# Hybrid decoder layer on one Trainium2 core: a second query block computed in the opening, every third low part made by GpSimd, modulation pieces and column sums placed at other points

## Chip, cores and metric

The kernel runs on 1 core of one Trainium2 chip. The metric is the device time of one execution in microseconds (us), lower is better. The kernel before was timed in three runs; their median is the number to compare with.

## What is computed

One decoder layer for 256 positions (SEQ) of width 2048 (D), all in f32. A conditioning vector `c` gives six vectors of 2048 (shift, scale and gate of the first norm, then of the second) through a matrix `w_ada` of 2048 x 12288, which is 96 MB. This modulation is the part that the change is most about.

```python
mod = (silu(c) @ w_ada + b_ada)
sh1, sc1, g1, sh2, sc2, g2 = split(mod, 6)
h = rmsnorm(x, norm1_g) * (1.0 + sc1) + sh1
sq, sk, sv, cq, ckv, kr = split(h @ w_in, IN_SPLITS)   # 1024, 1024, 1024, 512, 256, 64 columns
sb_out = stick_breaking_attention(sq, sk, sv)          # 8 heads of 128
q = rmsnorm(cq) @ w_uq;  kv = rmsnorm(ckv) @ w_ukv     # latent attention, 8 heads, 64 rotary columns
mla_out = mla_attention(q_nope, rope(q_pe), k_nope, rope(kr), v)
x = x + g1 * (concat(rmsnorm(sb_out), rmsnorm(mla_out)) @ w_o)
h2 = rmsnorm(x, norm2_g) * (1.0 + sc2) + sh2
x = x + g2 * peer_ffn(h2, ...)      # scores against keys, top 16 of 16384 experts for each of 8 heads
return rmsnorm(x, final_norm_g)
```

## The kernel before

Five engines each run a program written out by hand (one block per engine, from L675, L748, L846, L1244 and L1631 on), and wait for each other on semaphores. The order of the work is the order of the Python loops in these blocks: nothing is moved by a scheduler. TensorE (PE) multiplies, VectorE (DVE) and ScalarE (ACT) do elementwise work, SyncE (SP) and GpSimd (POOL) issue DMAs from their own queues. Eight banks of PSUM are handed out round by round with `plan`, `take`, `fill`, `full` and `empty` (L211 to L231). The stages are these.

**Opening (7 to 149 us).** Shift and scale of the first norm are needed ahead of any input product. Their part of `w_ada` comes as 64 pieces of 512 KB (`first_load`, L467, 14 buffers), 16 pieces for each quarter j of the columns. DVE adds them up, weighted by silu(c), in `first_acc` (`first_step`, L474 to L487). PE turns the sum of 128 partitions into columns by products with a vector of ones (`summed_columns`, L492, 8 matmuls for a quarter), and DVE and ACT apply them to the four 128-row chunks of `hT` of this quarter. Then PE multiplies the chunks, in whole f32, with the first input blocks, `OPENING = ("cq", "ckv", "q0")`: cq and ckv in L876, q0 in L882 (a block of 512 columns of `w_in`; each quarter comes in a tile `opened` of up to 1 MB). SP issues all these loads in one row: the opened tiles of a quarter with the 512 KB pieces of the next one between them.

**Input products (149 to 270 us).** The other blocks, q1, k0, k1, v0, v1, each have 8 pairs of chunks; a pair is counted by c (0 to 39). The weights come in halves of 2 MB in two ring slots (`load_half`, L360). f32 is split in two fp32r parts: ACT makes the high part (L448, four buffers `win_high`), DVE the low part, whole minus high (L452, 128x1024 at a time). PE then multiplies high part by high, weight high by `hT_low`, and weight low by `hT_high`: 24 matmuls of 256 columns for a pair of q or k (L912), 12 of 512 for a pair of v (L906). One record of the trace is one such matmul; a matmul in whole f32 has two records.

**The later modulation** (gate 1, shift 2, scale 2, gate 2) is pieces 32 to 95 of 1 MB, part = piece/16, in three buffers `ada_late` (the last three pieces in `ada_last`). The GpSimd queue issues them (`ada_load`, L302, DMA at L308); piece k waits until sum k-3 is done. DVE adds them up (`ada_sum`, L310; L319 for the first of a part, L322 for the others). PE sums the partitions when 16 pieces are done (`ada_cols(part)`, L329, matmuls L333, 16 for a part: 2 is gate 1, 3 is shift 2, 4 is scale 2), and DVE adds the bias (`ada_finish`, L339). At which points of DVE's program the sums stand is a table: `ada_after` (L513) for the input products, up to piece 58; then 59 to 63, and 64 to 70 (`ADA_IN = 71`) ahead of attention; 13 in the output products, at the pairs listed in the DVE block; the rest ahead of retrieval (`ADA_OUT = 86` is where the next list begins). `ada_cols(3)` stands behind the products `qpe` of the latent queries, `ada_cols(4)` in the output products, item 2, pair 2.

**Latent up-projections and attention (270 to 370 us).** `qpe` is rotated by DVE, then come scores, weights and values of 16 jobs on PE, ACT and DVE.

**Output products (370 to 461 us).** `w_o` in four items n of 8 pairs m, with the same split: high by ACT, low by DVE (L452), 12 matmuls of 512 for a pair (L1069), which is 2.72 us. `residual` (L1896, L1902, L1904) adds the result of the item before, twice in each item from 1 on. **Retrieval** is the rest, up to the end at 1749 us; the change does not touch it beyond the sums of modulation ahead of it.

## Time and profile before

| | |
|---|---|
| three runs | 1755.42, 1748.83, 1753.72 us |
| median | 1753.72 us |
| profiled execution, device time | 1751.18 us |
| its span (first to last instruction) | 1749.4 us |
| mean granted clock of TensorE | 0.909 of full speed |
| matmul, PE | 1478.3 us busy, 85% |
| VectorE | 1206.5 us busy, 69% |
| GpSimd | 690.7 us busy, 39% |
| ScalarE | 542.8 us busy, 31% |
| DMA | 624.46 MB in packets of the queues, mean 357 GB/s |

The profile is of one execution. Its times count from the span's start, and busy shares are means over all stages. GpSimd's time is nearly all in the gathers of the retrieval: before 520 us it does little but issue the modulation pieces. The granted clock is 1.00 where TensorE runs at 2.4 GHz. A row of the timeline joins instructions that follow each other; its last number in brackets is the idle time before them and what ended it.

### The profile page before, as it was taken

The numbers are of one execution on the slowest core, as the hardware profiler recorded it, in microseconds if no ns is written. First come the engines' busy times: TensorE is split into PE (matmuls) and PEld (weight loads), VectorE is DVE, ScalarE is ACT, GpSimd is POOL, SyncE is SP. The second block draws the span as 40 slices with busy tenths as digits, with TensorE's granted clock in tenths as the row PEclk, the third lists the DMA queues.
The fourth block names the chain that finished last, engine by engine and source line by source line (L and its number), as shares of the span: only waits on it lengthen the run. The fifth ranks groups of instructions, "written<-read, shape, count | busy, mean of one in ns | idle before, by whom it ended". The sixth has DMA issues, their size and how long they took to land.

```text
span 1749.4 us, 20157 instructions
## 1 busy us (share of the span) xinstructions
PE 1478.3 (85%) x7320; PEld 980.5 (56%) x7320; DVE 1206.5 (69%) x2134; ACT 542.8 (31%) x1589; POOL 690.7 (39%) x626
## 2 busy tenths in 40 slices
PE   2979999989999998898999757656689899988874
PEld 2558987878788875666676434324333343333331
DVE  5877886879889988898454467768654555445463
ACT  3003442764311247343210146537421010101132
POOL 1000011000122354556676466555654454445461
PEclk9889999999999999999999876667789999998987
DMA  9999997849969679999999899998989999999996
GB/s 337 386 385 407 402 354 308 303 167 370 380 233 359 225 293 379 377 368 397 390 402 396 325 388 379 378 350 319 394 338 406 366 402 400 362 417 389 416 381 249
DMA packets 149806, 624.46 MB, mean 357 GB/s; under 512 B 33994, under 2 KB 38272, under 8 KB 86528
## 3 DMA queue, kind: packets, MB, share of 16 engines
q0 software_dynamic: 82976, 427.52, 62.6%
q1 hardware_dynamic: 66732, 195.67, 29.1%
q8 instruction: 58, 0.95, 0.2%
q14 instruction: 40, 0.33, 0.0%
HBM read 797.54 MB, written 2.10 MB: 457 GB/s over the span
## 4 chain that ended last, share of the span: by engine, by line
PE 31%; DMA 30%; DVE 24%; issue 6%; POOL 5%; ACT 3%; DVEq 1%; SPq 1%; POOLq 0%; ACTq 0%
DMA u_rows<-in_peer_u,expert 23%; DVE u_rows L2033 12%; PE ps L1167 6%; PE ps L1069 5%; PE ps L457 4%; PE ps L912 4%; DVE first_acc L486 3%; DMA v_rows<-in_peer_v,expert_rows 3%; POOL v_rows L801 3%; PE ps L906 2%; PE ps L1219 2%; PE ps L1134 2%; DMA ada_first<-in_w_ada 2%; PE ps L1204 2%; DMA u_rows<-in_peer_v,expert_rows 1%
## 5 line engine op out<-in xcount | busy, mean ns | idle before, releaser
L2033 DVE SCALAR_TENSOR_TENSOR u_rows<-u_rows,h 128x1024 f32<-128x1024 f32 (+1 forms) x416 | 595.3, 1469 | 377.9 <-DMA u_rows<-in_peer_u,expert 374.3
L801 POOL DMA_INDIRECT u_rows<-in_peer_u,expert x256 | 320.6, 1253 | 364.5 <-DVE u_rows L2033 289.5
L801 POOL DMA_INDIRECT v_rows<-in_peer_v,expert_rows x199 | 264.1, 1327 | 162.3 <-PE ps L1167 108.5
L1167 PE MATMUL ps<-v_rows,diag 128*32 128x512 f32 x1592 | 259.4, 693 | 65.1 <-DMA v_rows<-in_peer_v,expert_rows 35.6
L1219 PE MATMUL ps<-dense_rows,dense_weight 128*128 128x512 f32 x640 | 290.6, 612 | 14.9 <-DVE dense_sums L2112 8.2
L457 PE MATMUL ps<-h2T,dense_rows 128*128 128x256 f32 x1280 | 284.0, 383 | 4.2 <-ACT dense_weight L1565 4.1
L457 PEld LDWEIGHTS ps<-h2T,dense_rows 128*128 128x128 f32 x1280 | 243.4, 191 | 52.6 <-issue 17.9
L1219 PEld LDWEIGHTS ps<-dense_rows,dense_weight 128*128 128x128 f32 x640 | 123.1, 196 | 181.9 <-issue 174.9
L1167 PEld LDWEIGHTS ps<-v_rows,diag 128*32 128x32 f32 x1592 | 64.9, 125 | 182.5 <-issue 182.0
L308 POOL DMA_DIRECT2D ada_late<-in_w_ada x61 | 32.4, 531 | 303.7 <-DVE ada_acc L322 260.8
L1204 PE MATMUL ps<-high_hot,low_hot 128*128 128x40 f32 x512 | 82.1, 332 | 78.7 <-issue 54.0
L322 DVE SCALAR_TENSOR_TENSOR ada_acc<-ada_late,cact,ada_acc 128x2048 f32<-128x2048 f32 x57 | 133.8, 2348 | 18.8 <-DMA ada_late<-in_w_ada 17.7
L1167 PE MATMUL ps<-spare_rows,diag 128*32 128x512 f32 x296 | 135.7, 673 | 9.7 <-DMA v_rows<-in_peer_v,expert_rows 9.7
L1204 PEld LDWEIGHTS ps<-high_hot,low_hot 128*128 128x128 f32 x512 | 78.9, 244 | 95.0 <-issue 95.0
L1134 PE MATMUL ps<-h2T,ring 128*128 128x256 f32 x512 | 114.2, 383 | 0.0
L1134 PEld LDWEIGHTS ps<-h2T,ring 128*128 128x128 f32 x512 | 97.4, 192 | 13.0
L1487 ACT ACTIVATE hidden<-hidden 128x16 f32<-128x16 f32 x15 | 3.2, 215 | 314.6 <-DVE hidden L2041 311.5
L1576 ACT ACTIVATE low_hot<-iota,slot_rows 128x128 f32<-128x128 f32 x256 | 78.1, 387 | 41.1 <-PE ps L1204 40.9
L486 DVE SCALAR_TENSOR_TENSOR first_acc<-ada_first,cact,first_acc 128x1024 f32<-128x1024 f32 x60 | 77.0, 1284 | 16.1 <-DMA ada_first<-in_w_ada 10.8
L1509 ACT COPY weight_rows<-kept 32x4 f32<-32x4 f32 x240 | 47.1, 196 | 109.4 <-DVE kept L2058 106.7
L1561 ACT ACTIVATE diag<-ident,weight_rows 128x32 f32<-128x32 f32 x256 | 58.6, 308 | 40.0 <-PE ps L1167 39.4
L448 ACT CAST win_high<-ring 128x1024 fp32r<-128x1024 f32 x40 | 41.8, 1052 | 74.4 <-DMA ring<-in_w_in 32.0
(308 smaller groups left out, 1874.1 us busy)
## 6 DMA issues: line engine op xcount, KB each, us to landing
ada_late<-in_w_ada POOLq DMA_DIRECT2D x61, 1024.0 KB, 7.8
dense_rows<-in_dense_u SPq DMA_DIRECT2D x40, 1024.0 KB, 8.9
dense_rows<-in_dense_v SPq DMA_DIRECT2D x40, 1024.0 KB, 9.0
ada_first<-in_w_ada SPq DMA_DIRECT2D x64, 512.0 KB, 11.6
ring<-in_w_in SPq DMA_DIRECT2D x10, 2048.0 KB, 23.8
ring<-in_w_o SPq DMA_DIRECT2D x8, 2048.0 KB, 16.8
ring<-in_w_peer_q SPq DMA_DIRECT2D x8, 2048.0 KB, 13.8
opened<-in_w_in SPq DMA_DIRECT2D x8, 1024.0 KB, 13.0
```

Source lines behind the costliest of these rows:

```text
L322: nc.vector.scalar_tensor_tensor(out=a, in0=piece, scalar=cact[:, kc:kc + 1], in1=a, op0=ALU.mult, op1=ALU.add).then_inc(ada_steps, 1)
L457: ins = nc.tensor.matmul(half, lhs(k), rhs(k), start=(k == 0), stop=(k == kc - 1))
L486: nc.vector.scalar_tensor_tensor(out=a, in0=piece, scalar=cact[:, kc:kc + 1], in1=a, op0=ALU.mult, op1=ALU.add).then_inc(first_steps, 1)
L801: nc.gpsimd.indirect_dma_start(buf[:, :], None, table, bass.IndirectOffsetOnAxis(ap=places, axis=0), bounds_check=last_sparse, oob_is_err= ...
L912: ins = nc.tensor.matmul(banks[b // 2][:, T * (b % 2):T * (b % 2) + T], w.of(part, k, P * b, P), h[:, ch, :], start=first and b % 2 == 0, ...
L1069: ins = nc.tensor.matmul(banks[t], mixed[:, h, P * t:P * t + P], w.of(part, k), start=h % H == 0 and part is w.high and mixed is mix_high_ ...
L1134: ins = nc.tensor.matmul(bank[:, T * s:T * s + T], ring[item[name][0]][:, lo:lo + P], h2T[:, ch, :], start=(ch == 0 and s == 0), stop=(ch ...
L1167: ins = nc.tensor.matmul(ps[rows, k, :], diag[n % len(diag)][:, :], v_slot(n)[0][:, 512 * k:512 * k + 512], start=first, stop=last)
L1204: ins = nc.tensor.matmul(o, low_hot[i % 2][:, k, :], high_hot[i % 2][:, k, :], start=True, stop=True)
L1219: ins = nc.tensor.matmul(ps[:, 4 + t, :], weight_tile(PIECE * m + a)[:, P * t:P * t + P], rows[:, 512 * a:512 * a + 512], start=m == 0 and ...
L1576: ins = nc.scalar.activation(hot[:, k, :], iota128[:, :], ACT.Abs, scale=-1.0, bias=slot_rows[:, 1, BATCH * b + k:BATCH * b + k + 1])
L2033: ins = nc.vector.scalar_tensor_tensor(out=u_rows[b][:, lo:hi], in0=u_rows[b][:, lo:hi], scalar=1.0, in1=h2[:, q // H, lo:hi], op0=ALU.mul ...
```

## The change

1. **q1 joins the opening** (`OPENING`), in four more tiles `opened_late` that lie in ring slot 0 (loaded as one 1 MB piece per quarter). The list of items with high and low parts is then k0, k1, v0, v1: 32 pairs, c from 0 to 31.
2. **One 512-column product for k.** `hT_high` and `hT_low` lie side by side in `h_parts`. For a pair of k, the high part of the weights is multiplied with both at once (8 matmuls of 512 columns), the low part with `hT_high` alone (8 of 256). The two halves of the result lie in one bank, four banks for an item; DVE adds them with a tensor_reduce (`heads_out`, 8 in all), in place of ACT's copies.
3. **Every third low part by GpSimd** (`by_gpsimd(c)`: c % 3 == 2), 10 of the 32 in the input products and 10 in the output products. GpSimd's queue has the loads of the modulation pieces between them (`load_behind`).
4. **Column sums of the second shift** (`ada_cols(3)`) go from behind `qpe` into the output products, behind pair 3 of item 0. `ada_cols(4)` goes from (2, 2) to (2, 6).
5. **Modulation sums elsewhere**: 62 instead of 71 is the first sum that is not made ahead of attention; 20 stand in the output products where 13 stood; the two that are left over (62, 63) stand ahead of them, and 12 where 10 were ahead of retrieval.
6. Smaller moves: the arguments of sine and cosine go from the first quarter of the sums to the second; the latent norm steps come earlier; the last two squares of the heads' norm go behind the first two output pairs; the column sums of all quarters share the free end of ckv's bank.

```diff
+    h_parts = at("h_parts", A + 112 * KB, [P, 2, KC, T], F32R)
+    hT_high, hT_low = h_parts[:, 0, :, :], h_parts[:, 1, :, :]
+    opened_late = [at(f"opened_late{j}", A + 8 * KB * j, [P, 2048]) for j in range(4)]
...
-    OPENING = ("cq", "ckv", "q0")
+    OPENING = ("cq", "ckv", "q0", "q1")
...
+    def by_gpsimd(c):
+        return c % 3 == 2
+
+    def low_made(eng, c, done, before):
+        if by_gpsimd(c):
+            eng.wait_ge(gpsimd_low, before + sum(map(by_gpsimd, range(c + 1))))
+        else:
+            eng.wait_ge(done, sum(not by_gpsimd(b) for b in range(c + 1)))
...
+        def make_low_on_gpsimd(self, pool, high_made):
+            pool.wait_ge(high_made, self.c + 1)
+            nc.gpsimd.tensor_tensor(self.low, self.whole, self.high.bitcast(F32), ALU.subtract).then_inc(gpsimd_low, 1)
...
-    ADA_IN, ADA_OUT = 71, 86
-    ada_after = {c: (37 + (c - 4) * 11 // 18, 37 + (c - 3) * 11 // 18) for c in range(4, 22)}
-    ada_after.update({c: (48 + (c - 25) * 11 // 15, 48 + (c - 24) * 11 // 15) for c in range(25, 40)})
+    ADA_IN, ADA_OUT = 62, 84
+    ada_after = {c: (35 + c * 13 // 22, 35 + (c + 1) * 13 // 22) for c in range(22)}
+    ada_after.update({c: (48 + (c - 25) * 5 // 7, 48 + (c - 24) * 5 // 7) for c in range(25, 32)})
+
+    ada_sites = [(0, 5), (0, 6), (0, 7)] + [(1, m) for m in (0, 1, 1, 2, 2, 3, 3, 6, 7)] + [(2, m) for m in (0, 1, 2, 3)] + [(3, m) for m in range(4)]
...
                 if j < 3:
-                    for i in range(9, KC):
+                    for i in range(12, KC):
                         first_load(sp, KC * (j + 1) + i)
...
+            for n in range(4):
+                for m in range(PAIRS):
+                    load_behind(done, summed)
+                    done = summed
+                    if by_gpsimd(PAIRS * n + m):
+                        Pair(f"w_o{n}", PAIRS * n + m, m, wo_high).make_low_on_gpsimd(pool, w_high)
+                    summed += ada_sites.count((n, m))
...
+                                if part is w.high:
+                                    ins = nc.tensor.matmul(banks[b].rearrange("p (s n) -> p s n", s=2), w.of(part, k, P * b, P),
+                                                           h_parts[:, :, ch, :], start=first, stop=False, skip_group_check=True)
+                                else:
+                                    ins = nc.tensor.matmul(banks[b][:, 0:T], w.of(part, k, P * b, P), hT_high[:, ch, :],
+                                                           start=False, stop=last, skip_group_check=True)
...
-            ada_cols(3)
             w = group(pe, "w_ukv", 2 * n_in, KVR // P)
...
+                    if n == 0 and m < 2:
+                        squares(JOBS - 2 + m)
                     if n == 0 and m == 1:
                         gate_rows()
-                    if n == 2 and m == 2:
+                    if n == 0 and m == 3:
+                        ada_cols(3)
+                    if n == 2 and m == 6:
                         ada_cols(4)
...
+            def heads_out(name, b):
+                dst = sbq if name[0] == "q" else sbk
+                parts = full(dve, f"{name}_{b}").rearrange("p (s n) -> p n s", s=2)
+                empty(nc.vector.tensor_reduce(dst[:, 4 * int(name[1]) + b, :], parts, AX.X, ALU.add), f"{name}_{b}")
...
-            ada_sums(59, 64)
+            ada_sums(53, ADA_IN)
...
-            ada_finish(3)
-            ada_sums(64, ADA_IN)
...
-                    Pair(f"w_o{n}", PAIRS * n + m, m, wo_high).make_low(dve, w_high, w_low)
+                    if not by_gpsimd(PAIRS * n + m):
+                        Pair(f"w_o{n}", PAIRS * n + m, m, wo_high).make_low(dve, w_high, w_low)
...
-                    if (n, m) in ((1, 0), (1, 1), (1, 2), (1, 6), (1, 7), (2, 0), (2, 1), (2, 6), (2, 7), (3, 0), (3, 1), (3, 2), (3, 3)):
+                    if (n, m) == (0, 5):
+                        ada_finish(3)
+                    for _ in range(ada_sites.count((n, m))):
                         ada_sum(next(ada))
```

PE at the end of the opening, before: `opened2` is the tile of q0, then the first pair of q1 in parts (`win_high`, `ring_low`).

```order
L882 MATMUL ps<-hT_56,opened2_0_81 128x256 x16
L498 MATMUL ps<-ones_165,first_acc1_78 128x1 x8
L876 MATMUL ps<-opened0_1_82,hT_56 128x512 x8
L876 MATMUL ps<-opened1_1_83,hT_56 128x320 x8
L882 MATMUL ps<-hT_56,opened2_1_84 128x256 x16
L912 MATMUL ps<-hT_high_58,win_high0_59 128x256 x4
L912 MATMUL ps<-hT_low_57,win_high0_59 128x256 x4
L912 MATMUL ps<-hT_high_58,win_high0_59 128x256 x4
L912 MATMUL ps<-hT_low_57,win_high0_59 128x256 x4
L912 MATMUL ps<-hT_high_58,ring_low0_119 128x256 x8
```

The same place on PE after the change; `opened_late` is the tile of q1, L924 is the former L882, and `h_parts` holds both parts of hT.

```order
L924 MATMUL ps<-hT_56,opened2_0_84 128x256 x16
L924 MATMUL ps<-hT_56,opened_late2_80 128x256 x16
L523 MATMUL ps<-ones_168,first_acc1_77 128x1 x8
L918 MATMUL ps<-opened0_1_85,hT_56 128x512 x8
L918 MATMUL ps<-opened1_1_86,hT_56 128x320 x8
L924 MATMUL ps<-hT_56,opened2_1_87 128x256 x16
L924 MATMUL ps<-hT_56,opened_late3_81 128x256 x16
L955 MATMUL ps<-h_parts_57,win_high0_58 128x512 x8
L958 MATMUL ps<-h_parts_57,ring_low1_123 128x256 x8
L955 MATMUL ps<-h_parts_57,win_high1_59 128x512 x8
```

q1 stands in each quarter behind q0, and the first pairs in parts are those of k0, with a product of 512 columns and one of 256 where three of 256 stood.

DVE in the output products before, item 1, pairs 0 to 5: low parts of the weights (L452), modulation sums (L322), and the three instructions of a residual.

```order
L452 TENSOR_TENSOR ring_low1_120<-ring1_50,wo_high0_123 128x1024
L322 SCALAR_TENSOR_TENSOR ada_acc_91<-ada_late2_87,cact_170,ada_acc_91 128x2048
L452 TENSOR_TENSOR ring_low1_120<-ring1_50,wo_high1_124 128x1024
L322 SCALAR_TENSOR_TENSOR ada_acc_91<-ada_late0_85,cact_170,ada_acc_91 128x2048
L452 TENSOR_TENSOR ring_low1_120<-ring1_50,wo_high2_125 128x1024
L322 SCALAR_TENSOR_TENSOR ada_acc_91<-ada_late1_86,cact_170,ada_acc_91 128x2048
L452 TENSOR_TENSOR ring_low1_120<-ring1_50,wo_high3_126 128x1024
L452 TENSOR_TENSOR ring_low1_120<-ring1_50,wo_high0_123 128x1024
L1896 SCALAR_TENSOR_TENSOR tmpo_127<-ps,rs_g_176,tmpo_127 128x512
L1902 TENSOR_TENSOR tmpo_127<-tmpo_127,g1b_117 128x512
L1904 TENSOR_TENSOR x2_54<-x2_54,tmpo_127 128x512
L452 TENSOR_TENSOR ring_low1_120<-ring1_50,wo_high1_124 128x1024
```

DVE after the change, from the sum in item 0, pair 6, to item 1, pair 3; L471 is the former L452, L320 and L323 the former L319 and L322, L1932 the former L1874 (low part of the mixed heads).

```order
L323 SCALAR_TENSOR_TENSOR ada_acc_94<-ada_late0_88,cact_173,ada_acc_94 128x2048
L1932 TENSOR_TENSOR mix_low_part_125<-mix_95,mix_high_part_124 128x512
L471 TENSOR_TENSOR ring_low0_122<-ring0_49,wo_high3_129 128x1024
L323 SCALAR_TENSOR_TENSOR ada_acc_94<-ada_late1_89,cact_173,ada_acc_94 128x2048
L323 SCALAR_TENSOR_TENSOR ada_acc_94<-ada_late2_90,cact_173,ada_acc_94 128x2048
L471 TENSOR_TENSOR ring_low1_123<-ring1_50,wo_high1_127 128x1024
L323 SCALAR_TENSOR_TENSOR ada_acc_94<-ada_late0_88,cact_173,ada_acc_94 128x2048
L323 SCALAR_TENSOR_TENSOR ada_acc_94<-ada_late1_89,cact_173,ada_acc_94 128x2048
L471 TENSOR_TENSOR ring_low1_123<-ring1_50,wo_high2_128 128x1024
L323 SCALAR_TENSOR_TENSOR ada_acc_94<-ada_late2_90,cact_173,ada_acc_94 128x2048
L323 SCALAR_TENSOR_TENSOR ada_acc_94<-ada_late0_88,cact_173,ada_acc_94 128x2048
L323 SCALAR_TENSOR_TENSOR ada_acc_94<-ada_late1_89,cact_173,ada_acc_94 128x2048
```

Sums stand in item 0 already, two stand at each of the pairs 1 to 3 of item 1 where one stood or none, and one low part in three is missing.

GpSimd in the output products after the change; before, it had only the DMAs of this queue there (L308, one after the other).

```order
L475 TENSOR_TENSOR ring_low0_122<-ring0_49,wo_high1_127 128x1024
L309 DMA ada_late2_90<-in_w_ada 128x2048
L309 DMA ada_late0_88<-in_w_ada 128x2048
L309 DMA ada_late1_89<-in_w_ada 128x2048
L475 TENSOR_TENSOR ring_low1_123<-ring1_50,wo_high0_126 128x1024
L309 DMA ada_late2_90<-in_w_ada 128x2048
L309 DMA ada_late0_88<-in_w_ada 128x2048
L309 DMA ada_late1_89<-in_w_ada 128x2048
L309 DMA ada_late2_90<-in_w_ada 128x2048
L309 DMA ada_late0_88<-in_w_ada 128x2048
L475 TENSOR_TENSOR ring_low1_123<-ring1_50,wo_high3_129 128x1024
```

The low parts (L475) now stand in one row with the issues of the pieces (L309), so each waits for what is ahead of it.

## Rows read from the trace of the kernel before

**Rows 1.** page, part 1: busy us, share of the span, instructions

```profile
PE 1478.3 (85%) x7320; PEld 980.5 (56%) x7320; DVE 1206.5 (69%) x2134; ACT 542.8 (31%) x1589; POOL 690.7 (39%) x626
```

**Rows 2.** windows: engines' busy us, granted clock, DMA share, GB/s

```profile
110.00:120.00 10.00, 8.62 (x39) 6.97 (x37) 9.27 (x8) 0.00 (x0) 0.00 (x0) 1.00 1.05 387
120.00:130.00 10.00, 4.86 (x18) 4.29 (x19) 5.83 (x9) 2.18 (x4) 2.16 (x4) 0.64 1.06 383
...
410.00:420.00 10.00, 10.00 (x45) 8.25 (x45) 8.07 (x6) 3.79 (x4) 1.06 (x2) 1.00 1.02 408
```

**Rows 3.** timeline of PE, opening: start us, us, what, idle before

```profile
66.94 1.95 PE L498 MATMUL ps<-ones,first_acc 128*128 128x1 f32 x16 [0.34 <-DVE first_acc L486]
...
123.55 3.57 PE L498 MATMUL ps<-ones,first_acc 128*128 128x1 f32 x16 [4.93 <-DVE first_acc L486]
128.72 13.53 PE L876 MATMUL ps<-opened,hT 128*128 128x512 f32 x32 [1.59 <-DVE hT L1732]
142.08 7.07 PE L882 MATMUL ps<-hT,opened 128*128 128x256 f32 x32
```

**Rows 4.** chain that ended last, in order: start us, us, what

```profile
149.15 66.23 PE ps L912 x552
215.38 3.84 PE ps L333 x32
...
224.55 43.65 PE ps L906 x191
...
297.21 5.21 DMA ada_late<-in_w_ada
...
375.05 46.31 PE ps L1069 x204
...
515.55 3.66 PE ps L333 x32
```

**Rows 5.** timeline of all engines, entry to attention

```profile
310.86 0.49 ACT L1363 ACTIVATE za<-ps 128x384 f32<-128x384 f32 x1
...
312.93 0.55 DVE L1810 SCALAR_TENSOR_TENSOR za<-za 128x384 f32<-128x384 f32 x1
```

**Rows 6.** timeline of DVE, output products

```profile
384.65 2.35 DVE L322 SCALAR_TENSOR_TENSOR ada_acc<-ada_late,cact,ada_acc 128x2048 f32<-128x2048 f32 x1
386.92 1.22 DVE L452 TENSOR_TENSOR ring_low<-ring,wo_high 128x1024 fp32r<-128x1024 f32 x1
388.05 2.35 DVE L322 SCALAR_TENSOR_TENSOR ada_acc<-ada_late,cact,ada_acc 128x2048 f32<-128x2048 f32 x1
...
395.98 0.75 DVE L1896 SCALAR_TENSOR_TENSOR tmpo<-ps,rs_g,tmpo 128x512 f32<-128x512 f32 x1
...
398.10 1.22 DVE L452 TENSOR_TENSOR ring_low<-ring,wo_high 128x1024 fp32r<-128x1024 f32 x1
...
414.69 2.35 DVE L322 SCALAR_TENSOR_TENSOR ada_acc<-ada_late,cact,ada_acc 128x2048 f32<-128x2048 f32 x1 [1.93 <-DMA ada_late<-in_w_ada]
...
426.87 1.28 DVE L319 TENSOR_SCALAR ada_acc<-ada_late,cact 128x2048 f32<-128x2048 f32 x1
```

**Rows 7.** timeline of POOL, same stage: a piece is issued

```profile
405.12 0.53 POOL L308 DMA_DIRECT2D ada_late<-in_w_ada  x1 [10.50 <-DVE ada_acc L322]
```

**Rows 8.** timeline of all engines, two stretches of retrieval

```profile
651.73 0.99 POOL L801 DMA_INDIRECT v_rows<-in_peer_v,expert_rows  x1 [0.30 <-issue]
652.94 2.29 DVE L2033 SCALAR_TENSOR_TENSOR u_rows<-u_rows,h 128x2048 f32<-128x2048 f32 x1 [4.02 <-DMA u_rows<-in_peer_u,expert]
653.02 3.07 POOL L801 DMA_INDIRECT v_rows<-in_peer_v,expert_rows  x1 [0.30 <-issue]
```

**Rows 9.** timeline of POOL, its elementwise instructions at the start

```profile
4.01 0.29 POOL L765 TENSOR_SCALAR_AFFINE_SELECT mask_sb<-mask_sb 128x128 f32<-128x128 f32 x1
```

**Rows 10.** timeline of DVE, start of retrieval

```profile
500.19 0.69 DVE L1999 TENSOR_REDUCE halves<-ps 128x32 f32<-128x512 f32 x1
...
501.06 7.26 DVE L322 SCALAR_TENSOR_TENSOR ada_acc<-ada_last,cact,ada_acc 128x2048 f32<-128x2048 f32 x3
```

More of the change, by code:

```diff
@@ L327, in ada_sums, with ada_bank @@
             ada_sum(k)
+    def ada_bank(part):
+        return ps[:, 3 if part == 2 else 7, :]
     def ada_cols(part):
@@ L342, in ada_finish @@
         lo, hi = KC * part, KC * part + KC
-        nc.vector.tensor_tensor(modc[:, lo:hi], ps[:, 7, lo:hi], vcA[:, 32 + lo:32 + hi],
+        nc.vector.tensor_tensor(modc[:, lo:hi], ada_bank(part)[:, lo:hi], vcA[:, 32 + lo:32 + hi],
                                 ALU.add).then_inc(ada_bias, 1)
@@ L859, in _ @@
                 fill(ins, f"xT{u}")
+            banks = {name: [take(pe, f"{name}_{i}") for i in range(2)] for name in OPENING}
             summed_columns(0)
-            banks = {name: [take(pe, f"{name}_{i}") for i in range(2)] for name in OPENING}
             for j in range(4):
@@ L876, in _ @@
                                 ins = nc.tensor.matmul(banks[name][t][:, 0:width], hT[:, ch, P * t:P * t + P], w[:, ch % 4, 0:width],
-                                                       start=(ch == 0), stop=last)
+                                                       start=(ch == 0 and (name, t) != ("ckv", 0)), stop=last, skip_group_check=True)
                                 if last:
@@ L890, in _ @@
                     summed_columns(j + 1)
-            for n, (name, _, width) in enumerate(IN_ITEMS[3:]):
-                banks = [take(pe, f"{name}_{i}") for i in range(2)]
+            for n, (name, _, width) in enumerate(IN_ITEMS[4:]):
+                banks = [take(pe, f"{name}_{i}") for i in range(2 if name[0] == "v" else 4)]
                 for m in range(PAIRS):
@@ L1034, in _ @@
             pe.wait_ge(emptied[6], before_retrieval[6])
-            for k in range(JOBS + 6):
+            for k in range(JOBS + 4):
                 for stage, j in steps(k, (0, scores), (6, squares), (4, values), (2, middle)):
@@ L1062, in _ @@
                         pe.wait_ge(mix_low, 2 * m + 2)
-                    pe.wait_ge(w_low, w.c + 1)
+                    low_made(pe, w.c, w_low, sum(map(by_gpsimd, range(IN_PAIRS))))
                     products = [(part, k, mixed) for part, mine in ((w.high, (mix_high_part, mix_low_part)), (w.low, (mix_high_part,)))
```

189 lines of the change are left out of this document (104 added, 85 removed).

## The prediction

> **What bounds the kernel now.** I read four views in this order. The page gives TensorE (PE) 85% of the span busy and VectorE (DVE) 69% [rows 1]; these are averages, and the change touches only the first 520 us, so I went on by stage. The windows show two regimes. In the opening (7 to 149 us) DMA is full, share 1.05 at 387 GB/s, while PE idles in places and its granted clock falls to 0.64 on average over 120 to 130 us [rows 2]; in that window the column sums, 16 records, take 3.57 us, where the same 16 took 1.95 at 66.94, after no idle time to speak of [rows 3]. So the opening is bound by bytes. From 149 us on, the chain runs through PE without a gap: 552 records of L912 in 66.23 us, which is 0.120 us each, 191 of L906 in 43.65, 0.2285 each, and in the output products 204 of L1069 in 46.31, 0.227 each [rows 4]. There PE bounds, and DVE is the cover that has little room. Behind 520 us nothing is changed; I carry the shift through to the end one for one.
>
> **The sum.** Times are on the axis of the profiled execution: span 1749.4 us, device time 1751.18, which is 2.5 below the median 1753.72 of the three runs.
>
> *Opening.* q1 joins cq, ckv and q0: three more 1.05 MB loads stand ahead of the last piece of the first modulation sums. At 387 GB/s [rows 2] they take 3.15/387 = 8.2 us. PE computes q1 in whole f32: one group of the size of q0's, 7.07 us [rows 3], per quarter. For the first three quarters it lies in PE's idle time (a quarter had 28 us and gets 31); the fourth is on the path: +7.0. With PE nearly without idle, the columns should take 1.95 instead of 3.57: -1.6. The moved sine arguments cost DVE the same as before and lie under the loads; if DMA were not the bound they would cost or give some 4 us. Together **+13.6**.
>
> *Input products.* q1 leaves: 192 records x 0.120 = **-23.0**. In k0 and k1, two 256-column products with the high part become one of 512 columns. No q or k product of before has that form; L906 at 0.2285 is nearest, against 2 x 0.120, so a pair falls from 2.88 to 2.79 us: 16 pairs, **-1.5** (bounds 0 and -3.0, a quarter to either side). The eight copies by ScalarE become eight reductions by DVE; L1999 reduces 512 columns of PSUM in 0.69 [rows 10]: 5.5 us of DVE, hidden if DVE keeps ahead. It does, alone: from the end of the opening to the last low part it has 17 sums (16 of 2.27 and one of 1.19: 37.5; from start to start, a sum is 384.65 to 386.92 and a low part 386.92 to 388.05, and both rows are 0.08 to 0.09 longer [rows 6]), 19 low parts of 1.13 (21.5), 5.5 of reductions and, estimated, 4 of small things, 68.5, in PE's 92.
>
> *Entry to attention.* The 16 columns of the second shift, 3.5 us of PE [rows 4], leave this place: **-3.5**. Attention began when DVE had done its seven sums, at 312.93; ScalarE's scores were ready at 310.86 + 0.49 [rows 5]: **-1.6**. What is late next is the nine sums ahead of the rotation of q; at about 3.5 us each (an estimate: 2.27 and a wait for a piece) they end some 5 us ahead of PE's need. If not, PE waits there.
>
> *GpSimd's low parts.* No row has this instruction. Below, it could not beat DVE's own 1.13 [rows 6]; above, the one elementwise GpSimd row that reads SBUF, 0.29 for 128 columns [rows 9], gives 8 x 0.29 = 2.35 for 1024. I take 2.35, since it also reads. What matters is whom it blocks. A gather of GpSimd took 0.99 us when DVE was idle, and 3.07 when a DVE instruction with two SBUF inputs began just before it: that ended at 655.23, the gather 0.86 later [rows 8]. So GpSimd waits for such an instruction to its end. DVE's sums and low parts are all of that kind, and I assume the reverse: DVE stands for the 2.35. Then a low part given away costs DVE 2.35 instead of 1.13. In the input products, nine times 2.35 is 21.2 against 23 of room: **+4** (0 to 8).
> The Trainium skill, SBUF — State Buffer, Who interferes with whom, states this rule against the change: a DVE instruction with two SBUF inputs contends with a GpSimd one that reads SBUF, and the first to start blocks the other throughout. The trace agrees for the one direction it shows. The skill's GPSIMD Engine Reference, 3.1, has 4497 ns for a tensor_tensor of 2048 columns; an estimate from that, half, is 2.25, and would take about 0.8 us off the next term.
>
> *Output products.* The columns of the second shift come behind pair 3 of the first item: PE is there at 375.05 + 2 x 2.72 = 380.5 (a pair is 12 records of 0.227), and done at 384.0. DVE can't begin piece 64 before. From then to the last low part the order asks of DVE: 20 sums (18 of 2.27, two of 1.19 [rows 6]: 43.2), 18 low parts (20.3), 6 residuals of three instructions, from 395.98 to 398.10 (12.7), 1.2 of the last low parts of the mixed heads (estimate); with 8 low parts of GpSimd (18.8) that is 96.2 us, to 480.2, and 3.2 of products behind it: 483.4. Before, the stage ended, by the same pace, at 375.05 + 30 x 2.72 and some 4.4 us of other products on PE: 461.1. That is +22.3, and 2.7 for waits on pieces: **+25** (19 to 44), the moved columns included.
>
> *Start of retrieval.* Two more sums: they end at 501.06 + 7.26 + 4.7 = 513.0, and the columns that release the gathers stand on PE at 515.55 [rows 4, 10]. Covered by 2.5 us: **+1**.
>
> Sum: 13.6 - 23.0 - 1.5 - 3.5 - 1.6 + 4 + 25 + 1 = **+14.0**, hence 1765.2 for the profiled execution and 1767.7 for the median.
>
> **The rivals.**
> *Second: the port costs DVE nothing, but the order does.* Three buffers carry the pieces, and a piece is issued when the sum three before it is done. With a weight load in flight it landed late: issued at 405.12, its sum began at 414.69 [rows 6, 7], 9.5 us. Sum 64 ends at 385.2; 67 then ends at 385.2 + 9.5 + 2.3 = 397.0, 70 at 408.8, 73 at 420.6, and the low part of pair 12, queued behind it, at 421.7. PE wants it at 384.0 + 8 x 2.72 = 405.8. Wait: 15.9; with the columns +19.4 (up to 27 if the next six sums also run at 3.9). Total +14.0 - 4 - 25 + 19.4 = **+4.4**, 1758 (to 1766). For it: DMA is already full in this stage [rows 2] and seven more pieces come into it. Against it: it takes the low parts of GpSimd as free.
> *Third, faster.* GpSimd's lows block nobody, and pieces land as one did at 297.21, in 5.21 us [rows 4]. Then DVE's own work up to that low part is 28.5 us (to 412.5): PE waits 6.7. The sum is 14.0 - 4 - 25 + 3.5 + 6.7 - 1 = -5.8, and -12.5 if even that finds cover: **-9**, 1745. It decides where a piece lands in under 6 us and the input and output low parts of DVE keep 1.13. Against it: 20 sums where 13 were, DMA already full there.
> *Fourth.* GpSimd's blocking and late pieces in series, both at their upper bounds (8 and 44): **+37**, 1791.
>
> **How the numbers follow.** A measurement of this kernel can tell about 0.5%, 8.8 us. I give 0.44 to the forecast (0.38 slower, 0.06 within, where its small ends meet), 0.27 to the second (0.19 within, 0.08 slower), 0.24 to the third (0.20 faster, 0.04 within), 0.05 to the fourth. Together 0.20 faster, 0.29 same, 0.51 slower. The range runs from the third case (1743) to just under the fourth (1790).
>
> **What would show it.** Right: the last first_acc ends near 132; products of v1 end near 261 (257 without the port); DVE's sums or low parts that overlap a GpSimd low part show 3 to 5 us or gaps of 2.3; in the second item of the output products PE waits for DVE or GpSimd by 15 us or more; that stage lasts 25 us longer. Wrong: POOL's low part and DVE's sum side by side at their full speeds; or PE without a gap from 384 on this axis; or an opening that does not grow by 8 us.

## The result

| | before | after |
|---|---|---|
| median of the runs | 1753.06 us (4 runs) | 1775.19 us (4 runs, 1772.81 to 1778.39) |
| profiled execution, device time (span) | 1751.18 (1749.4) us | 1776.0 (1773.2) us |
| ratio after to before, 95% interval | | 1.0127 (1.0100 to 1.0155) |

The change makes the kernel 1.3% slower: 22 us where 14 were forecast, inside the range. (The fourth run of before came with the changed kernel and moves the median of before from 1753.72 to 1753.06.) The page of the changed kernel, part 1, answers to [rows 1]: GpSimd is 54 us busier, and VectorE is busier too, by 5.9 us, although it makes 28 low parts fewer (20 are GpSimd's now, 8 are gone with q1) and only the eight reductions of k, 5.4 us, more.

```profile
PE 1488.5 (84%) x7128; PEld 977.8 (55%) x7128; DVE 1212.4 (68%) x2114; ACT 533.3 (30%) x1577; POOL 745.1 (42%) x646
```

The best map of a change like this is a row of points that every variant has, read from the timeline of PE: the first product in parts (the opening's end), the first product of `cqT` with a weight (the input products' end), the first product of `za` with `tri` (attention runs), the first product of `wo_high` (output products start), the first transposes of `xs` (they are done), the last column sums, of the second gate (they release the gathers, but for the first three). All in us from the span's start; the last column is the time from there to the span's end, where all kernels run the same instructions.

| kernel | opening ends | input products end | attention | output products start | done | last column sums | to the end |
|---|---|---|---|---|---|---|---|
| before | 148.80 | 271.03 | 315.79 | 363.35 | 466.30 | 515.38 | 1234.0 |
| after | 162.36 | 263.87 | 303.60 | 351.17 | 488.45 | 538.69 | 1234.5 |
| e1, no GpSimd low parts | 162.81 | 257.65 | 297.38 | 344.97 | 472.83 | 522.72 | 1239.4 |
| e2, GpSimd in input only | 163.81 | 270.40 | 310.12 | 357.71 | 485.88 | 539.09 | 1233.3 |
| e3, GpSimd in output only | 162.51 | 259.13 | 300.27 | 347.82 | 485.12 | 535.42 | 1241.6 |
| e10, two thirds by GpSimd | 163.03 | 278.68 | 318.41 | 365.97 | 508.77 | 560.95 | 1234.5 |
| e4, before with GpSimd | 148.70 | 271.94 | 316.85 | 364.44 | 470.73 | 519.92 | 1238.3 |
| e6, low part first | 163.12 | 263.94 | 304.17 | 351.71 | 490.56 | 542.74 | 1235.2 |
| e7, before with new places | 147.45 | 269.39 | 309.11 | 356.66 | 486.27 | 535.52 | 1235.8 |
| e5, sums in the idle time | 162.89 | 262.79 | 318.57 | 366.11 | 473.06 | 522.51 | 1242.7 |
| e8, rotation first | 163.18 | 258.01 | 303.16 | 351.10 | 454.54 | 503.87 | 1234.9 |
| e9, best places | 162.71 | 260.56 | 305.63 | 353.21 | 460.23 | 509.57 | 1229.1 |

Between before and after, all stages but one stand where the prediction put them. Up to the start of the output products the change gains 12.2 us; the output products last 137.3 us where they lasted 103.0, and lose 34.3. The windows show how. Before, PE is busy without a pause at the full clock (the columns are PE, PEld, DVE, ACT and POOL busy, granted clock, DMA share, GB/s):

```profile
390.00:420.00 30.00, 30.00 (x134) 24.82 (x133) 27.93 (x23) 14.02 (x17) 3.18 (x6) 1.00 1.04 382
420.00:450.00 30.00, 30.00 (x150) 25.38 (x150) 28.73 (x25) 11.31 (x15) 3.18 (x6) 1.00 0.95 369
```

After, PE is busy two thirds and four fifths of the same windows at a granted clock of 0.83 and 0.89, with DVE at 26 and 29 of 30 us: DVE sets the pace.

```profile
390.00:420.00 30.00, 20.18 (x70) 14.66 (x69) 26.25 (x17) 7.20 (x11) 8.55 (x9) 0.83 1.04 395
420.00:450.00 30.00, 24.52 (x94) 19.09 (x93) 29.09 (x17) 10.15 (x14) 11.26 (x8) 0.89 0.94 356
```

The last column varies from 1229.1 to 1242.7 us, although the instructions are the same there and only the head start of the first gathers differs. Kernels of the same head start (e1, e2, e3, e5: VectorE's first product with gathered rows stands within 0.6 us of the column sums) still range from 1233.3 to 1242.7. A single execution's total is therefore not read to the microsecond below; where a few us matter, the stages are compared, and these too are those of one execution for each kernel. The input products alone, without any low part by GpSimd, take from 94.8 (e1, e8) to 99.9 us (e5).

PE's waits tell where the 34.3 us of the output products went. From 351 to 484 us PE waits for low parts:

```profile
PE ps L1115 <- POOL ring_low L475: 11.7, 3, 5.9
PE ps L1115 <- DVE ring_low L471: 10.0, 6, 4.5
```

That is 21.7 us where it waited 3.4 before. Two sets of column sums in place of one are 5.0 more, and what remains, some 11 us, is products at the lower clock (next section).

### The profile page after: what moved, and what is told of

Read it like the earlier page. It is cut to its first block, busy times and chain, and to the rows that moved or that the text cites. A ratio compares the mean times of both kernels' runs of the same rounds, so it can differ in the third digit from the quotient of the medians.

```text
span 1773.2 us, 19763 instructions
## 1 busy us (share of the span) xinstructions
PE 1488.5 (84%) x7128; PEld 977.8 (55%) x7128; DVE 1212.4 (68%) x2114; ACT 533.3 (30%) x1577; POOL 745.1 (42%) x646
## 4 chain that ended last, share of the span: by engine, by line
DMA 33%; DVE 25%; PE 24%; issue 8%; POOL 5%; ACT 3%; DVEq 1%; SPq 0%; POOLq 0%; ACTq 0%
DMA u_rows<-in_peer_u,expert 20%; DVE u_rows L2094 10%; PE ps L1217 6%; PE ps L1269 6%; DMA v_rows<-in_peer_v,expert_rows 5%; PE ps L480 4%; DVE ada_acc L323 3%; POOL v_rows L844 3%; DMA ada_first<-in_w_ada 3%; PE ps L1115 2%; PE ps L948 2%; DVE first_acc L511 2%; DMA ada_late<-in_w_ada 2%; DMA ring<-in_w_in 1%; POOL u_rows L844 1%
## 5 line engine op out<-in xcount | busy, mean ns | idle before, releaser
L844 POOL DMA_INDIRECT u_rows<-in_peer_u,expert x256 | 327.6, 1280 | 368.7 <-DVE u_rows L2094 294.6
L844 POOL DMA_INDIRECT v_rows<-in_peer_v,expert_rows x199 | 256.7, 1290 | 158.1 <-PE ps L1217 104.6
L1217 PE MATMUL ps<-v_rows,diag 128*32 128x512 f32 x1592 | 261.1, 695 | 63.9 <-DMA v_rows<-in_peer_v,expert_rows 37.9
L323 DVE SCALAR_TENSOR_TENSOR ada_acc<-ada_late,cact,ada_acc 128x2048 f32<-128x2048 f32 x57 | 141.4, 2482 | 20.9 <-DMA ada_late<-in_w_ada 19.4
L309 POOL DMA_DIRECT2D ada_late<-in_w_ada x61 | 33.1, 542 | 251.8 <-DVE ada_acc L323 223.4
L1115 PE MATMUL ps<-wo_high,mix_high_part 128*128 128x512 f32 x128 | 46.3, 443 | 21.7 <-POOL ring_low L475 11.7
## 6 DMA issues: line engine op xcount, KB each, us to landing
ring<-in_w_o SPq DMA_DIRECT2D x8, 2048.0 KB, 15.2
```

The source lines that it names most:

```text
L323: nc.vector.scalar_tensor_tensor(out=a, in0=piece, scalar=cact[:, kc:kc + 1], in1=a, op0=ALU.mult, op1=ALU.add).then_inc(ada_steps, 1)
L844: nc.gpsimd.indirect_dma_start(buf[:, :], None, table, bass.IndirectOffsetOnAxis(ap=places, axis=0), bounds_check=last_sparse, oob_is_err= ...
L1115: ins = nc.tensor.matmul(banks[t], mixed[:, h, P * t:P * t + P], w.of(part, k), start=h % H == 0 and part is w.high and mixed is mix_high_ ...
L1217: ins = nc.tensor.matmul(ps[rows, k, :], diag[n % len(diag)][:, :], v_slot(n)[0][:, 512 * k:512 * k + 512], start=first, stop=last)
```

## What held GpSimd and VectorE apart, in the changed kernel's rows

The timeline of all engines in the input products, then later in the output products:

```profile
169.50 2.50 POOL L475 TENSOR_TENSOR ring_low<-ring,win_high 128x1024 fp32r<-128x1024 f32 x1
169.66 2.37 DVE L1755 TENSOR_SCALAR st<-st 128x2 f32<-128x2 f32 x1
...
180.96 2.55 POOL L475 TENSOR_TENSOR ring_low<-ring,win_high 128x1024 fp32r<-128x1024 f32 x1
...
181.16 2.43 DVE L1831 COPY kpad<-kpad 128x128 f32<-128x128 f32 x1
```

```profile
401.65 2.35 POOL L475 TENSOR_TENSOR ring_low<-ring,wo_high 128x1024 fp32r<-128x1024 f32 x1
...
404.05 1.22 PE L1115 MATMUL ps<-wo_high,mix_high_part 128*128 128x512 f32 x2 [5.88 <-POOL ring_low L475]
...
409.45 2.55 POOL L475 TENSOR_TENSOR ring_low<-ring,wo_high 128x1024 fp32r<-128x1024 f32 x1
409.66 0.74 DVE L1954 SCALAR_TENSOR_TENSOR tmpo<-ps,rs_g,tmpo 128x512 f32<-128x512 f32 x1
...
410.44 2.11 DVE L1960 TENSOR_TENSOR tmpo<-tmpo,g1b 128x512 f32<-128x512 f32 x1
...
410.90 0.62 PE L1115 MATMUL ps<-wo_high,mix_high_part 128*128 128x512 f32 x2
```

GpSimd's low part takes 2.35 to 2.59 us undisturbed, a little over the estimate of 2.35; 5 of the 20 last longer, 3.0 to 3.9. What DVE begins beside it mostly stands until it ends: at 169.66 a TENSOR_SCALAR of two columns takes 2.37 us and ends with GpSimd's 2.50 (169.50), at 181.16 a copy of 128 columns takes 2.43, at 410.44 a product of 512 columns that elsewhere takes 0.69 takes 2.11. The row at 409.66 is the counter-example: L1954 reads PSUM and one tile of SBUF, starts 0.21 after GpSimd, and takes its 0.74. So it is not every DVE instruction that waits, and not only those with two SBUF inputs: the copy and the TENSOR_SCALAR have one. The Trainium skill, SBUF — State Buffer, Who interferes with whom, says just that: `copy` and `tensor_scalar` within SBUF can take the shared ports too, and an instruction with at most one SBUF input outside those modes does not contend; the rows agree.

The block goes the other way too. These rows are from the same timeline:

```profile
379.20 4.80 DVE L323 SCALAR_TENSOR_TENSOR ada_acc<-ada_late,cact,ada_acc 128x2048 f32<-128x2048 f32 x2
382.39 3.83 POOL L475 TENSOR_TENSOR ring_low<-ring,wo_high 128x1024 fp32r<-128x1024 f32 x1
383.92 3.38 DVE L471 TENSOR_TENSOR ring_low<-ring,wo_high 128x1024 fp32r<-128x1024 f32 x1
```

GpSimd's low part begins under a sum that ends at 384.00 and ends 2.2 us behind it; DVE's next low part then stands until GpSimd is done.

The rows at 404.05 also show the second price. There PE resumes after 5.88 us of waiting for GpSimd's low part, and a run of two products takes 1.05 to 1.22 us where 0.62 is the rule (410.90). The granted clock over this pair (404.05 to 409.33) is 0.54, so it ran almost wholly at the lower of the two levels, 1.2 GHz. Four more pairs of this stage have a granted clock of 0.50 to 0.66: the one behind the wait of 3.85 us at 430.29, one behind 1.81 us at 393.87 that slows half-way, and the two behind column sums (371.91 and 455.59). Such a pair lasts 4.2 to 5.3 us where others last 2.72, together 10 us more. Not every pause or column sum is followed by one: behind 1.95 us at 386.36 the clock is 1.00, and so it is in the kernel before, behind its column sums at 421.20.

## The experiments

Theories. **P** (mine): GpSimd's low parts block VectorE for longer than they relieve it. **O**: GpSimd is free for VectorE; the order of sums and pieces costs. **Q**: the low parts are late because they queue behind issues. **D/R**: the places of the sums cost by themselves, because VectorE idles ahead of them and has no room behind.

### e1 to e3: GpSimd's low parts taken away, in all and in each stage

```diff
     def by_gpsimd(c):
-        return c % 3 == 2
+        return False
```

e2 and e3 have a rule for each stage, `c % 3 == 2` in one and `False` in the other.

e1. 

> Theory P (GpSimd's low parts block VectorE): VectorE gets 20 low parts of 1.13 us back and loses 20 blocks of 2.3 to 2.6 us. In the output products six of them stand between 372 and 448 us, where VectorE sets the pace: minus 6 x 1.2 to 1.4 = 7 to 8 us, and some of the lower clock behind PE's gaps with it. In the input products PE's four gaps (4.0 us) close. Together 10 to 14 us shorter than the changed kernel, 1761 to 1765. Theory O (only the order of the sums costs; GpSimd's work is free for VectorE): VectorE has 22.6 us more to do, so 1775 (same) to 1790.

e2. 

> GpSimd makes low parts in the input products alone. P: the output products' share comes back, 7 to 10 us shorter than the changed kernel, 1765 to 1768. O: same to slower, 1775 to 1783.

e3. 

> GpSimd makes low parts in the output products alone. P: the input products' share comes back, 3 to 5 us shorter than the changed kernel, 1770 to 1772. O: same to slower, 1775 to 1783. If the costs add, this gain and that of the kernel with GpSimd in the input products alone make that of the kernel without any.

Measured, median and ratio to before: e1 1764.59, 1.0077 (1.0045 to 1.0109); e2 1776.68, 1.0132 (1.0103 to 1.0160); e3 1775.89, 1.0121 (1.0090 to 1.0152). e1 is 10.6 us under the changed kernel's median (9 by the ratios, whose intervals leave 1 to 16), which P had (10 to 14) and O had not. In the totals, e2 and e3 give nothing back: both lie in O's range (1775 to 1783), P's 1765 to 1768 and 1770 to 1772 missed, and the sum rule that I had written (the parts add) fails. In the stages P holds for the output products: 137.3 us with GpSimd's low parts (after and e3 alike), 127.9 and 128.2 without (e1, e2), so 9 us. In the input products PE waits for low parts 4.0 us in the changed kernel and 9.8 in e2, and not at all in e1 and e3. So 4 to 10 us are the low parts' there. The stages' own lengths (101.5 and 106.6 against 94.8 and 96.6) hold the granted clock too, which is 0.94 from 235 to 262 us in the changed kernel and 1.00 in e1; e5, without GpSimd, has 0.94 as well. In e2, PE waits for a DVE low part from the stage's first product on, then 3.1 us more for the last modulation sum ahead of the gathers. e3 releases the gathers 3.3 us before the changed kernel does and takes 7.1 more from there on, where the instructions are the same. Why six runs of each give nothing back in the median stays open. The low parts that DVE makes, from the groups of the tile `ring_low` (min/median/max in ns), in the changed kernel and in e1:

```profile
L471 DVE TENSOR_TENSOR ring_low<-ring,win_high x22: 1209/1216/3775, 155.9 to 252.1; 128x1024 fp32r<-128x1024 f32 x22
L471 DVE TENSOR_TENSOR ring_low<-ring,wo_high x22: 1212/1219/3421, 349.8 to 477.1; 128x1024 fp32r<-128x1024 f32 x22
```

```profile
L471 DVE TENSOR_TENSOR ring_low<-ring,win_high x32: 1211/1218/1226, 156.5 to 245.7; 128x1024 fp32r<-128x1024 f32 x32
L471 DVE TENSOR_TENSOR ring_low<-ring,wo_high x32: 1216/1218/1225, 343.6 to 461.7; 128x1024 fp32r<-128x1024 f32 x32
```

Without GpSimd, none of 64 lasts over 1226 ns; with it, single ones last 3.4 and 3.8 us.

### e10: two thirds by GpSimd, the suspected cost doubled

```diff
     def by_gpsimd(c):
-        return c % 3 == 2
+        return c % 3 != 0
```

> The changed kernel with two of three low parts by GpSimd in place of one. Theory P: the cost of the first third over none was 10.6 us; 21 or 22 more low parts at 1.2 to 1.4 us of VectorE each, and GpSimd's own queue as the second pace: 1787 to 1805. Rival (only the third that stands at the wrong pairs costs): 1775 to 1780.

Measured 1797.25 us, ratio 1.0223 (1.0198 to 1.0249): another 22 us, as P had it. The page's part 1 of e1 (no low part by GpSimd), then of e10 (42):

```profile
PE 1480.5 (84%) x7128; PEld 971.3 (55%) x7128; DVE 1202.8 (68%) x2134; ACT 533.6 (30%) x1577; POOL 696.9 (40%) x626
```

```profile
PE 1496.8 (83%) x7128; PEld 982.4 (55%) x7128; DVE 1228.7 (68%) x2092; ACT 533.4 (30%) x1577; POOL 817.4 (46%) x668
```

VectorE is busy 1202.8 us with 64 low parts of its own, 1212.4 with 44 (after), 1228.7 with 22. Had GpSimd been free, 20 low parts less would have made 1202.8 - 20 x 1.22 = 1178.4, and 42 less 1151.6. The difference is time in which VectorE stood blocked: 34.0 us for 20 and 77.1 for 42, 1.7 and 1.8 each, against the 1.22 that each takes off it. e2, e3 and e4 give the same by their pages (1207.8, 1207.4 and 1217.4 busy, with 10, 10 and 23 given away): 1.7 each; e6 (1207.8, with 20) gives 1.5. The block that P names is thus measured six times, and e10 shows that it costs time. That it is less than the 2.35 of the prediction, because some low parts fall where VectorE has nothing to do or reads PSUM, is my reading and not tested.

### e4: the kernel before with GpSimd's low parts

The changed kernel's `by_gpsimd`, `low_made`, `make_low_on_gpsimd` and `load_behind` in the kernel before, 13 and 10 low parts.

```diff
-                    Pair(name, c, m, win_high, width).make_low(dve, in_high, in_low)
+                    if not by_gpsimd(c):
+                        Pair(name, c, m, win_high, width).make_low(dve, in_high, in_low)
```

> The kernel before, with every third low part by GpSimd (13 in the input products, 10 in the output products) and the loads of the pieces between them, nothing else changed. P: 23 times 1.2 us more for VectorE, of which its idle time takes a part: 5 to 20 us slower than before, 1758 to 1773. O: 0 to 3 us faster, since VectorE is relieved of 23 low parts.

Measured 1758.07 us (12 runs), ratio 1.0028 (1.0009 to 1.0048): slower, as P says and O does not, but by 4 to 5 us, at or just under the low end of P's 5 to 20. The stages: input products 123.2 in place of 122.2, output products 106.3 in place of 103.0. GpSimd's instruction is the same (groups of `ring_low`):

```profile
L466 POOL TENSOR_TENSOR ring_low<-ring,win_high x13: 2400/2559/3866, 151.7 to 260.6; 128x1024 fp32r<-128x1024 f32 x13
L466 POOL TENSOR_TENSOR ring_low<-ring,wo_high x10: 2407/2644/4009, 365.2 to 451.9; 128x1024 fp32r<-128x1024 f32 x10
```

So the same offloading costs 4 us here, 1.0 and 3.3 in the two stages, where PE sets the pace, and 9.4 in the output products of the changed kernel (after against e1), where VectorE does. The price is the place's, not the instruction's.

### e6: the low part ahead of the issues in GpSimd's queue

```diff
-                    load_behind(done, summed)
-                    done = summed
                     if by_gpsimd(c):
                         Pair(name, c, m, win_high, width).make_low_on_gpsimd(pool, in_high)
+                    load_behind(done, summed)
+                    done = summed
```

(and the same in the output products)

> The changed kernel with GpSimd's low part of a pair ahead of the issues of the pieces, in place of behind them. Theory Q (the low part is late because it stands in GpSimd's queue behind an issue that waits for a VectorE sum): the two longest gaps of PE, 5.88 and 3.85 us, shrink, 1770 to 1772. Rival (VectorE's blocking is all of it, or the pieces are issued later and pay it back): same as the changed kernel, 1774 to 1778.

Measured 1780.58 us, ratio 1.0151 (1.0118 to 1.0184): no gain, and 2.6 us over the rival's range. Q falls. PE's long gaps remain. They now end with DVE's low part, which stands behind sums that wait longer for their pieces (6.7 us of waits in the output products, 3.9 in the changed kernel), as the rival's second half has it (timeline of PE):

```profile
395.68 1.22 PE L1115 MATMUL ps<-wo_high,mix_high_part 128*128 128x512 f32 x2 [4.69 <-DVE ring_low L471]
411.73 1.19 PE L1115 MATMUL ps<-wo_high,mix_high_part 128*128 128x512 f32 x2 [8.26 <-DVE ring_low L471]
```

### e7: the places alone, in the kernel before

The table `ada_sites`, `ADA_IN, ADA_OUT = 62, 84` and the places of `ada_cols(3)` and `ada_cols(4)` of the change, and nothing else.

```diff
-    ADA_IN, ADA_OUT = 71, 86
+    ADA_IN, ADA_OUT = 62, 84
...
-            ada_sums(59, 64)
+            ada_sums(59, ADA_IN)
...
-            ada_finish(3)
-            ada_sums(64, ADA_IN)
```

> The kernel before with the changed kernel's places for the modulation sums and the column sums of the second shift and scale alone (62 first in the output products, 20 sums there), q1 not in the opening, no GpSimd. Theory R (the places alone make the output products longer, since VectorE idles until the columns of the second shift and then has 20 sums and all low parts): output products plus 20 to 25 us, entry to attention minus 5: 1768 to 1774. Rival (the places cost only where q1 has left and the input products are shorter): 1749 to 1756.

Measured 1773.07 us, ratio 1.0117 (1.0093 to 1.0140), as R had it. Entry to attention is 5.0 us shorter (39.7 for 44.8) and the output products are 26.7 longer (129.6 for 103.0), a little over R's 20 to 25; the windows have the same look as after, without any low part by GpSimd:

```profile
390.00:420.00 30.00, 21.58 (x69) 16.40 (x68) 26.13 (x19) 7.80 (x11) 3.17 (x6) 0.77 1.03 397
420.00:450.00 30.00, 27.35 (x121) 20.95 (x119) 27.05 (x22) 12.53 (x17) 3.17 (x6) 1.00 1.03 404
```

The places alone make a loss of 20 us, nearly as much as the whole change. In the change the gain of q1's move stands against it and the cost of GpSimd's low parts comes on top; no run has q1's move alone.

### e5, e8, e9: the sums where VectorE idles

In e1, VectorE idles 8 us ahead of attention, 6.4 behind pair 1 of item 0 (it waits for the squares) and 5.8 behind pair 5 (it waits for the columns of the second shift), and is late for PE afterwards. e5 is e1 with the columns of the second shift ahead of attention and the sums in those gaps.

```diff
-    ADA_IN, ADA_OUT = 62, 84
+    ADA_IN, ADA_OUT = 66, 84
...
+            copied(pe, "v1_1")
+            ada_cols(3)
             pe.wait_ge(qpe_ready, 2)
...
-            ada_sums(53, ADA_IN)
+            ada_sums(53, 64)
...
+            ada_finish(3)
+            ada_sums(64, ADA_IN)
```

> The changed kernel without GpSimd's low parts, and with the modulation sums where VectorE was idle in it: the column sums of the second shift stand on PE behind the value products, ahead of attention; sums 62 to 65 ahead of attention, 66 and 67 ahead of the output products, three behind pair 1 of item 0, the rest spread over all items (16 there in place of 20), the columns of the second scale behind pair (2, 4). Theory D (VectorE's work fits into its idle time, the order decided): the output products last 103 to 107 us in place of 127.9, which makes 1744 to 1750, under both kernels. Rival (pieces land late, or the retrieval gives it back): 1755 to 1762.

Measured 1757.71 us (12 runs), ratio 1.0012 (0.9989 to 1.0036). The output products last 107.0, as D had it, and PE has no pause in these windows:

```profile
390.00:420.00 30.00, 30.00 (x134) 24.83 (x133) 29.86 (x24) 14.27 (x18) 2.77 (x6) 1.00 1.05 386
420.00:450.00 30.00, 30.00 (x136) 25.40 (x135) 25.74 (x22) 10.90 (x15) 2.51 (x5) 0.89 0.94 357
```

But the time is the rival's (1755 to 1762), because the loss moved. The trace is of the longest of the twelve runs, 1766.91 us; the shortest took 1743.99, so what it shows need not be as large in all of them. Timeline of PE, then of DVE, ahead of attention:

```profile
297.75 9.68 PE L480 MATMUL ps<-ring,ckvT 128*128 128x512 f32 x16 [7.14 <-DVE rt L1849]
307.27 4.57 PE L337 MATMUL ps<-ones,ada_acc 128*128 128x1 f32 x32
```

```profile
293.43 2.35 DVE L323 SCALAR_TENSOR_TENSOR ada_acc<-ada_late,cact,ada_acc 128x2048 f32<-128x2048 f32 x1 [2.92 <-DMA ada_late<-in_w_ada]
...
311.94 0.17 DVE L347 TENSOR_TENSOR modc<-ps,vcA 128x16 f32<-128x16 f32 x1 [11.30 <-PE ps L337]
```

PE's value products wait 7.14 us for the rotation of q, which stands on DVE behind eleven sums, and then run at a granted clock of 0.73 (9.68 where 7.03 is usual); the columns of the second shift come behind them, and DVE waits 11.30 us for these. e8 puts the rotation behind sum 60:

```diff
-            ada_sums(53, 64)
+            ada_sums(53, 61)
...
+            ada_sums(61, 64)
             ada_finish(3)
```

> The kernel with the sums in the idle time, and the rotation of q behind sum 60 in place of sum 63. Theory D (there PE's value products waited 7.14 us for the rotation, which stood behind eleven sums, and the columns of the second shift waited with them): attention begins 12 to 15 us earlier and the output products keep 107 us, 1743 to 1748. Rival (sum 63 is late in any case, since its pieces land late): PE waits the same at the columns, 1754 to 1760.

Measured 1746.66 us, ratio 0.9952 (0.9934 to 0.9970): inside D's range and faster than before. Attention begins 15.4 us earlier by the traces: 10.6 of them lie between the input products and attention, the rest in the input products, where the two kernels are alike. The medians differ by 11. e9 has one sum ahead of attention in place of two (behind the columns of the second shift) and 19 in the output products in place of 16, so that 10 are left for the retrieval.

> As the kernel with the rotation first, but one sum ahead of attention in place of two, and 19 sums in the output products in place of 16, so that 10 stand ahead of the retrieval as before. Theory D: the last sum ahead of the gathers ends 5 us earlier, and VectorE still fits into the output products: 1739 to 1745. Rival (VectorE has no room for three more sums there): output products 112 us or more, 1745 to 1752.

Measured 1743.80 us, ratio 0.9938 (0.9916 to 0.9961): 11.8 us under the runs of before on the same chip, and 31 under the changed kernel's median. Its output products last 107.0, so VectorE has room for the three sums. PE's value products no longer wait, and the columns of the second shift wait 0.85 us (timeline of PE):

```profile
288.23 7.03 PE L480 MATMUL ps<-ring,ckvT 128*128 128x512 f32 x16
296.11 3.70 PE L337 MATMUL ps<-ones,ada_acc 128*128 128x1 f32 x32 [0.85 <-DVE ada_acc L323]
```

e8 and e9 can't be told apart by these intervals, and what D gave as the reason for e9's gain isn't seen: the gathers are released 49.3 us behind the output products in both.

## Why the prediction was right, and where not

**Opening, +13.6.** Measured 162.36 - 148.80 = 13.6, but half for another reason. Timeline of PE:

```profile
72.02 3.57 PE L523 MATMUL ps<-ones,first_acc 128*128 128x1 f32 x16 [4.85 <-DVE first_acc L511]
...
104.13 1.84 PE L523 MATMUL ps<-ones,first_acc 128*128 128x1 f32 x16
...
134.05 1.84 PE L523 MATMUL ps<-ones,first_acc 128*128 128x1 f32 x16
137.49 11.41 PE L918 MATMUL ps<-opened,hT 128*128 128x512 f32 x32 [1.60 <-DVE hT L1786]
...
162.36 2.21 PE L955 MATMUL ps<-h_parts,win_high 128*128 128x512 f32 x8
164.41 1.11 PE L958 MATMUL ps<-h_parts,ring_low 128*128 128x256 f32 x8
165.35 2.00 PE L955 MATMUL ps<-h_parts,win_high 128*128 128x512 f32 x8
...
168.15 2.00 PE L955 MATMUL ps<-h_parts,win_high 128*128 128x512 f32 x8
```

The columns of the last two quarters (104.13, 134.05) show no idle time ahead of them and take 1.84, forecast 1.95. The last sums of the first modulation ended at 131.0 (forecast 132), 3 us before PE came for them: PE, not DMA, bounds the second half of the opening. I had bytes on the path for 8.2 us up to the last columns and 5.4 behind them. Measured are 10.5 (134.05 for 123.55) and 3.1, since PE's group of cq and ckv took 11.41 in place of 13.53, at the full clock. Two errors cancelled, so the total is partly luck.

**Input products, -20.5.** Measured 101.5 - 122.2 = -20.7. A pair of k lasts 2.80 us (165.35 to 168.15 above), forecast 2.79 from v's record. GpSimd's share, forecast +4 (0 to 8), is 4.0 by PE's waits; the stage is 6.7 longer than in e1, with the clock in it. The products of v1 ended at 261.1, forecast 261.

**Entry to attention, -5.1.** Measured 39.7 - 44.8 = -5.0. No wait for the rotation. The nine sums ended at 288.1, 3.4 us ahead of PE's value products at 291.54, where I had estimated 5; e3 waits 0.9 us there and e5 shows the price when the cover is gone.

**GpSimd's low part.** 2.35 assumed, 2.35 the least measured, 2.50 and 2.55 the medians of the two stages. That VectorE stands for it was assumed from the other direction; rows and e10 show it.

**Output products, +25 (19 to 44).** Measured +34.3; this is the term that was mis-sized. The step that failed is the one that ran DVE's time through "to the last low part" and put 3.2 us of products behind it. For the part in which DVE does set the pace, it was good: from the end of the second shift's columns at 372.05 to the last low part that PE waited for at 448.16 are 76.1 us; the same list of instructions, priced as in the prediction, is 16 sums, 12 low parts, 4 residuals, 1.2 and 6 low parts of GpSimd, 35.2 + 13.6 + 8.5 + 1.2 + 14.1 = 72.6, and 2.7 for pieces. (Measured, the six low parts of GpSimd hold VectorE for 12.5 us there, and it waits 3.9 for pieces.) But behind 448.16 four sums are left for ten pairs, and PE is the bound again, as the chain shows:

```profile
448.16 3.02 PE ps L1115 x12
451.18 4.55 PE ps L337 x32
455.73 24.05 PE ps L1115 x96
```

Ten pairs of 2.72, the second scale's columns of 4.6, key transposes, and a pair at the lower clock are 36 us. The prediction had 26.8 of DVE and products there. I had one engine's total for a stage in which the bound changes hands, and the columns of the second scale, which stand at (2, 6), in no term behind the point where PE takes over. The same account fits e1: from its columns' end at 365.9, the list without GpSimd (17 low parts) and 2.7 for pieces give 66.8 us; the last low part that PE waits for is there at 435.4, 69.5 behind, and 33 us of PE follow.

**Start of retrieval, +1.** The columns that release the gathers stand 23.3 later, the end of the output products 22.2: +1.2. The first three gathers, which wait for VectorE alone, are issued 28.6 later (529.97 for 501.41); from the output products to the span's end the kernels take 1284.8 and 1283.1, so little of that is seen in the total.

**The rivals.** The second took the port as free and found a loss in the order alone. The experiments give the order more than I did: it makes the output products 25 us longer without any block (e1 127.9, e7 129.6, before 103.0), and GpSimd adds 9.4 on top. My own sum for this stage, without GpSimd and with its 8 low parts on DVE, would have been +15.2 in place of +25, so it had the block's share right (9.8) and the order's 10 us too small. The rival had +19.4 (to 27) for the order, from late pieces; in e1 VectorE waits only 4.1 us for pieces in this stage, so the lateness that it named is a small part. In total it forecast +4.4; e1 measured +13.5 by the ratio, 10.5 by the medians. The third, faster, isn't borne out for this change, since GpSimd does block, and two pieces of the chain took 8.5 and 8.7 us to land where it needed under 6. Its gain from q1's move is there: with the sums well placed (e9) the kernel is 11 us faster than before, and opening and input products together are 10.5 shorter. No run has these places without q1's move.

**The signs.** The last `first_acc`, the end of v1's products, the opening's growth and DVE instructions of 3 to 5 us beside GpSimd came as named. Two did not: in the second item of the output products PE waits 11.8 us (1.95, 1.81, 5.88, 0.56 and 1.57), where 15 or more were named, and the stage grew by 34 us in place of 25.

## What to carry to other kernels

A change that shortens one engine's work also shortens the cover of another: before it is worth anything, the covered work (here the modulation sums that lay beside q1's 23 us) needs another place, and an engine that idles early in a stage can't pay that back later in it. Cost a stage in stretches, by the engine that is late in each, and not by one engine's total. Work given to GpSimd beside a full VectorE is not relief where they share SBUF ports: measure the blocked time (busy time with, less busy time without, plus what was moved) before counting the gain.
